# Retention mixer: decay tables made head by head in place, plain gate blocks at both ends, and query/key pairs in a row

## The reference

```python
q, k, v, g = jnp.split(a @ w_in, [hk, 2 * hk, 2 * hk + hv], axis=-1)
q, k = apply_rope(q, *rope), apply_rope(k, *rope)   # latent tokens
k = k * RET_DK ** -0.5
log_gamma = -jnp.exp(decay_param)                   # one per head and direction
o_ctx, o_lat = bidirectional_scan(ctx_terms, lat_terms)
y = rms_norm_2(o)
return (jax.nn.silu(g) * y) @ w_out
```

## Time and profile before

| what | value |
|---|---|
| median of 3 runs | 2966.15 us (2964.76 to 2968.64) |
| profiled execution, own time | 2970.24 us |
| its span, first to last instruction | 2968.4 us |
| mean granted TensorE clock | 0.971 |
| busy: PE, DVE, ACT, POOL | 94%, 68%, 43%, 12% |

### The profile page before, as it was taken

One profiled execution on the slowest core, in us unless ns is written; L12 is line 12 of the kernel. 1 busy time (PEld: TensorE's weight loads), 2 busy tenths in 40 slices (PEclk: granted clock), 3 DMA queues, 4 the chain that ended last, 5 costly groups with the idle time before them and its releaser, 6 DMA issues.

```text
span 2968.4 us, 42896 instructions
## 1 busy us (share of the span) xinstructions
PE 2782.5 (94%) x16374; PEld 2488.8 (84%) x16374; DVE 2023.3 (68%) x3722; ACT 1283.5 (43%) x2369; POOL 369.4 (12%) x207
## 2 busy tenths in 40 slices
PE   9999999999999399989997899999989998999998
PEld 8888987988888298978886889999977777989898
DVE  7788688769878567744546687666674435677676
ACT  5322357633235444432223634334446435554354
POOL 2243200124330000011110000000002222000000
PEclk9999999999999699999998999999989999999999
DMA  6556321256552333323321012222222121122322
GB/s 198 192 182 198 121 95 50 84 190 202 184 161 67 135 137 142 116 104 131 131 96 50 16 59 71 70 71 65 80 71 75 47 72 49 65 79 72 114 86 79
DMA packets 99613, 312.19 MB, mean 105 GB/s; under 512 B 10320, under 2 KB 25808, under 8 KB 97872
## 3 DMA queue, kind: packets, MB, share of 16 engines
q1 hardware_dynamic: 92208, 287.42, 29.7%
q10 hardware_dynamic: 7200, 22.02, 2.0%
HBM read 283.71 MB, written 24.12 MB: 104 GB/s over the span
## 4 chain that ended last, share of the span: by engine, by line
PE 51%; DVE 6%; ACT 2%; issue 1%; DMA 1%; POOL 0%; DVEq 0%; ACTq 0%; SPq 0%; POOLq 0%
PE ps L2248 16%; PE ps L2249 16%; PE ps L2250 16%; DVE t_wlo L2974 1%; PE ps L2531 1%; PE ps L2515 1%; PE ps L2504 1%; ACT t_whi L2574 1%; DVE t_x L3208 0%; DVE t_m L3208 0%; DVE t_m L3093 0%; DMA t_m<-s_dec 0%; DMA t_raw<-in_gu 0%; DVE t_x L3174 0%; DVE t_h L3214 0%
## 5 line engine op out<-in xcount | busy, mean ns | idle before, releaser
L2574 ACT CAST t_whi<-t_raw 128x512 fp32r<-128x512 f32 (+3 forms) x494 | 381.4, 783 | 671.5 <-PE ps L2250 457.4
L2248 PE MATMUL ps<-t_h,t_whi 128*128 128x256 f32 (+2 forms) x1852 | 628.3, 339 | 7.7 <-DVE t_wlo L2974 2.6
L2249 PE MATMUL ps<-t_h,t_wlo 128*128 128x256 f32 (+2 forms) x1852 | 623.6, 337 | 0.0
L2250 PE MATMUL ps<-t_h,t_whi 128*128 128x256 f32 (+2 forms) x1852 | 623.6, 337 | 0.0
L2974 DVE TENSOR_TENSOR t_wlo<-t_raw,t_whi 128x512 fp32r<-128x512 f32 (+3 forms) x420 | 356.9, 861 | 121.2 <-ACT t_whi L2574 116.7
L2248 PEld LDWEIGHTS ps<-t_h,t_whi 128*128 128x128 f32 x1852 | 354.7, 192 | 42.2 <-issue 9.9
L2249 PEld LDWEIGHTS ps<-t_h,t_wlo 128*128 128x128 f32 x1852 | 354.8, 192 | 26.1 <-issue 0.2
L2250 PEld LDWEIGHTS ps<-t_h,t_whi 128*128 128x128 f32 x1852 | 354.6, 191 | 26.3
L2248 PE MATMUL ps<-t_mw,t_whi 128*128 128x256 f32 (+2 forms) x922 | 299.3, 325 | 74.6 <-ACT t_tmp L2579 34.8
L2248 PE MATMUL ps<-t_hid,t_whi 128*128 128x256 f32 (+2 forms) x1032 | 335.5, 325 | 0.7 <-DVE t_hid L3273 0.6
L2249 PE MATMUL ps<-t_hid,t_wlo 128*128 128x256 f32 (+2 forms) x1032 | 333.6, 323 | 0.0
(11 more groups left out here) (373 smaller groups left out, 4962.5 us busy)
## 6 DMA issues: line engine op xcount, KB each, us to landing
t_raw<-in_gu SPq DMA_DIRECT2D x174, 512.0 KB, 3.4
t_raw<-in_ada SPq DMA_DIRECT2D x96, 512.0 KB, 3.6
t_raw<-in_dn SPq DMA_DIRECT2D x52, 512.0 KB, 4.2
t_raw<-in_dn SPq DMA_DIRECT2D x24, 384.0 KB, 3.4
s_qk<-t_hid ACTq DMA_DIRECT2D x12, 768.0 KB, 4.3
t_hid<-s_qk SPq DMA_DIRECT2D x6, 1536.0 KB, 11.6
t_raw<-in_ret_v SPq DMA_DIRECT2D x16, 512.0 KB, 4.8
t_raw<-in_ret_g SPq DMA_DIRECT2D x16, 512.0 KB, 3.8
```

Of the source, the lines that this page charges most:

```text
L2248: e.matmul(out, whi, xlo, start=first, stop=False, skip_group_check=shared)
L2249: e.matmul(out, wlo, xhi, start=False, stop=False, skip_group_check=shared)
L2250: return e.matmul(out, whi, xhi, start=False, stop=last, skip_group_check=shared)
L2574: e.copy(m.block(0, it.slot, n), m.raw(it)).then_inc(*S["hi"].of(j))
```

## The change

- One plain gate block (head 3, channel block 2) stays in front, where there were two; a second one (head 3, block 3) is multiplied behind head 3's last value product. Its silu (`g_late`) writes straight to the place of the gates, and head 3 loads three blocks of gates instead of four.
- Heads come in the order 1, 2, 3, 0, and of each first the two query/key pairs, then the gate pairs (head 3: one).
- No decay table is made in front, stored or loaded again. The distances are loaded (`dist_load`, 768 KB) straight into the table's place, and the table is made there: for head 0 while its gate pairs run, for head h+1 behind the last score of head h. The same operations run (two in another order), five on VectorE and three exps on ScalarE.
- The loads of rope, distances and values move from SyncE's queue to ScalarE's.
- The planner counts transfers as longer, the more so the larger they are (1.3 ns more for each element of a row over 1024), which shifts orders everywhere. In the program ScalarE has 51 table loads, before 40.

```diff
@@ schedule, the planner's costs
-            takes, lasts = 480, 3300
+            takes, lasts = 480, 3300 + 1.3 * max(n - 1024, 0)
...
@@ schedule, retention
-        def plain_gates(h, i):
+        def early_gate(h, c):
...
+        def late_gate(h, c, after):
+            def post(g):
+                put("g_late", h=h, c=c, g=g.id, bank=g.bank, t0=g.t0, n=g.n, after=after)
+            columns([(("ret_g", h * 4 + c), (SLOT,), DC, ("h", 4), [(0, "drain_act", post)])], SEG2[::-1])
...
                 if (t0, i) == (0, 1):
                     finish(h, 512, 256)
-                    gated_values(h, 512, 256)
+                    gated_values(h, 512, 256, range(4 if h < n_head - 1 else 3))
+            if h == n_head - 1:
+                from_bank(4)
+                late_gate(h, 3, ov["oc"])
+                gated_values(h, 512, 256, (3,))
             finish(h, 0, 512)
-            gated_values(h, 0, 512)
+            gated_values(h, 0, 512, range(4))
...
-        for h in range(n_head):
-            late = decays(h, late)
-        put("rope_load", after=[("ret_act", ("ll", n_head - 1))])
-        sides[:] = [late] * 4
-        plain_gates(1, 0)
+        put("rope_load", after=pro)
+        sides[:] = [pro] * 4
+        early_gate(n_head - 1, 2)
...
-        gate_pairs = [(1, 1), (2, 0), (2, 1), (3, 0), (3, 1), (0, 0), (0, 1)]
-        pairs = [(h, w) for h in (1, 2, 3, 0) for w in range(2)]
-        for k, (h, w) in enumerate(pairs):
-            seven_pair("qk", h, w)
-            if k != 3:
-                last = seven_pair("g", *gate_pairs[k - (k > 3)])
+        for h in (1, 2, 3, 0):
+            for w in range(2):
+                seven_pair("qk", h, w)
+            if h == 0:
+                rope_done = sides[0] + sides[1] + sides[2] + sides[3]
+                put("dist_load", h=0, after=rope_done)
+                put("ret_decay", h=0, after=rope_done)
+            for w in range(1 if h == 3 else 2):
+                last = seven_pair("g", h, w)
...
-        put("dec_load", h=0, after=rope_done + [("d_ds", n_head - 1)])
         put("v_load", after=[("ps", last["P6"])])
...
             attend(h)
+            if h < n_head - 1:
+                put("dist_load", h=h + 1, after=[("drain_dve", ("ret_p", h, 0, 5))])
+                put("ret_decay", h=h + 1, after=[("p_lo", (h, 0, 5))])
...
-            from_bank(4)
+            if h < n_head - 1:
+                from_bank(4)
@@ ScalarE
-        e.activation(ll, ta, ACT.Exp).then_inc(*S["ret_act"].of(("ll", h)))
+        e.activation(ll, ll, ACT.Exp).then_inc(*S["ret_act"].of(("ll", h)))
         yield
-        e.activation(gs, d2, ACT.Exp, scale=m.sm(8 + h, 1)).then_inc(*S["ret_act"].of(("g1", h)))
-        e.activation(tb[:, 0:640], d2, ACT.Exp, scale=m.sm(4 + h, 1), bias=m.sm(20 + h, 1)).then_inc(*S["ret_act"].of(("g2", h)))
...
+    def g_late(it):
+        w.wait_ge("ps", it.g)
+        wait_all(it.after)
+        e.activation(m.ret_gate(it.c, it.t0, it.n), m.PS[:, it.bank, 0:it.n], ACT.Silu).then_inc(*S["drain_act"].of(it.g, ("g_late", it.t0)))
```

More of the change, by code:

```diff
@@ L319, in arrange @@
                     end = op.due
-        self.heads_on = next(op.item.id for op in self.ops["sync"] if op.item.kind == "ret_setup")
+        self.heads_on = next(op.item.id for op in self.ops["scalar"] if op.item.kind == "ret_setup")
         return self.run(families)
@@ L1375, in retention @@
         ov, t, sides, staged, stores = {}, {}, [[], [], [], []], {}, {h: [] for h in range(n_head)}
[L1377 to L1381, removed]
         def v_rows(h):
@@ L1516, in finish, with gated_values @@
             put("ret_recip", h=h, t0=t0, n=n)
-        def gated_values(h, t0, n):
-            for c in range(4):
+        def gated_values(h, t0, n, some):
+            for c in some:
                 put("ret_y", h=h, c=c, t0=t0, n=n)
@@ L1557, in retention @@
                 state["h_free"] = [("ps", max(it.id for it in items if it.kind == "group"))]
-                put("dec_load", h=h + 1, after=[("drain_dve", ("ret_p", h, 0, 5))])
                 put("qk_load", h=h + 1, after=[("ret_ps", ("s", h, 0, 5))] + [staged[w] for w in range(2)])
             else:
+                state["h_free"] = [("ps", max(it.id for it in items if it.kind == "group"))]
                 state["acc_free"] = [("p_lo", (h, 0, 5)), ("drain_dve", ("ret_p", h, 0, 5))]
@@ L2183, in serve @@
             e.dma_start(m.at(MMASK, 256), dram["mask1"]).then_inc(*S["d_misc"].of("mask1"))
[L2184 to L2206, removed]
         elif it.kind == "qk_load":
@@ L2813, in ret_decay, with dist_load, v_load, rope_load @@
     def ret_decay(it):
[L2814 to L2815 removed]
+        h = it.h
+        ll, gs, tb = m.at(RST, 896), m.at(RST + 896, 640), m.at(RPA, 896)
         w.wait_ge("ret_dve", ("d3", h))
         wait_all(it.after)
[L2818 removed]
+        e.activation(ll, ll, ACT.Exp).then_inc(*S["ret_act"].of(("ll", h)))
         yield
[L2820 to L2826 removed]
+        e.activation(tb[:, 0:640], gs, ACT.Exp, scale=m.sm(4 + h, 1), bias=m.sm(20 + h, 1)).then_inc(*S["ret_act"].of(("g2", h)))
+        w.wait_ge("ret_act", ("g2", h))
+        e.activation(gs, gs, ACT.Exp, scale=m.sm(8 + h, 1)).then_inc(*S["ret_act"].of(("g1", h)))
+    def dist_load(it):
+        wait_all(it.after)
+        e.dma_start(m.at(RST, 1536), dram["dist"]).then_inc(*S["d_dist"].of(it.h))
+    def v_load(it):
+        wait_all(it.after)
+        w.wait_ge("d_vs0", 0)
+        for part in range(2):
+            o, src = (RVV, RVL)[part], dram["s_v"][part]
+            e.dma_start(m.MW[:, o + 2048:o + 3072].bitcast(F32), src[:, 2048:3072]).then_inc(*S["d_rv0"].of(("part", part), 0))
+        for part in range(2):
+            o, src = (RVV, RVL)[part], dram["s_v"][part]
+            e.dma_start(m.MW[:, o:o + 2048].bitcast(F32), src[:, 0:2048]).then_inc(*S["d_rv1"].of(("part", part), 0))
+    def rope_load(it):
+        wait_all(it.after)
+        e.dma_start(m.at(RCS, 1024), dram["rope"]).then_inc(*S["d_ret"].of("rope"))
     def v_store(it):
```

60 lines of the change are left out of this document (29 added, 31 removed).

## The result

The changed kernel takes 2778.7 us (median of 4 runs, 2777.8 to 2781.4) against 2967.2 us before; the ratio is 0.9367, with an interval of 0.9351 to 0.9383. Forecast were 2891 us and a range of 2864 to 2917. The direction was right, the size was not: −188.5 us for −75.

A forecast was written before the change was run, and what follows sets the result against it. TensorE's work (94% of the span) plus its gaps was taken to bound the kernel; −55 − 9 + 0 − 11 = −75 us from 2970.2 gave 2895, less 4.1: 2891 us, range 2864 to 2917.

The forecast's parts named there:

- What bounds the kernel: Whole kernel: time is TensorE's work, 94% of the span, plus its gaps; waits looked at around the retention mixer.
- drift: Rival, whole program: new transfer costs in the planner shift orders, 11 more table loads; +5 to +14 us; chance 0.08.
- Term 1 and 2: Start of the input products, −55 us, and first scores of head 0, −9 us.
- rows of two: Input products: two query/key pairs in a row cost TensorE time, 4 us for all four places.
- term 2: First scores of head 0: table made in place ends an 8.4 us wait, about 1 us may stay; −9 us.
- decay chain: First input pair: snap copies stand behind the decays, a 29.13 us gap that goes when four decays and stores go.
- Term 3: Inside the heads: decay work delays y by 6 to 8 us, but this is covered; 0, up to +12 us.
- cover: Inside the heads: TensorE runs the next head's value rows meanwhile, hiding a delay of 6 to 8 us.
- Term 4: End of head 3: rest of the output product starts earlier, with the moved gate block paid; −11 us (−27 to 0).
- The table loads: Switches of table counted at 1.28 us each, without the skill's drain of about 1380 ns; with it, 2894 us.

The follow-up runs named there:

- e1: Kernel before, planner's walk following only waits and the order inside a family, so due times reach every operation; 2808.8 us, ratio 0.9463.
- e3: Kernel before, with the two loads of the distances issued by ScalarE instead of SyncE, which removes the planner's circle; 2795.9 us, ratio 0.942.
- e2: Changed kernel, with due times carried back only through as many operations as in the kernel before (7287); 2920.6 us, ratio 0.9842 to the kernel before.
- e6: Changed kernel with the planner's old, flat cost of transfers; 2780.1 us.
- e4: Changed kernel with both plain gate blocks of head 3 in front and no late block; 2770.6 us, ratio 0.9336.
- e7: Changed kernel with both plain gate blocks in front and query/key and gate pairs in turn; 2769.0 us, ratio 0.9327.
- e9: Kernel before, with the distances and also the reloads of the decay tables on ScalarE's queue; 2793.8 us.

## Why the prediction was wrong, step by step

- **What bounds the kernel** was half read. That TensorE's gaps decide was right, but I looked for their causes only in the stretch that the diff names, took the waits of the FFN and the attention for given, and put them into the sum at nothing. They were 88.3 us, the largest error. e1 and e3 bring all of it with the due times and none of the other edits, and e2 loses all but 5 us of it with nothing but the due times cut.
- **What the terms are worth with the old due times** is read from e2, which has every edit. Up to the first sum it is 46.5 us ahead of the kernel before (1282.2 to 1235.7), for a forecast of 64; one gap of 24.96 us is left in the first pair, for low parts of weights (L2979). The end of head 3 is 3.0 us longer (90.3 to 93.3), for a forecast of −11. In all it is 47 us for 75. So the right direction at these places was earned, but the time there comes near the forecast, or beyond it, only together with the due times, and that is luck.
- **The step that failed** is the rival "drift": the planner's part was priced as a loss of 5 to 14 us, and for the wrong cause, its costs of transfers (e6: nothing) and the table loads. That an edit can change whether the planner knows any due time was not asked. The planner's part was a gain, of 142 us (e2, beside all the other edits) to 159 (e1, without them) or 172 (e3, with the distances early as well). The order of ScalarE quoted ahead of the prediction had the sign of it: 24 in-place scalings stood ahead of the casts and the silu that TensorE was waiting for.
- **Term 1 and 2**, −64 us for the way to the first head: measured −81.0 up to its first sum. P1 starts at 955.52 us (forecast 958.9; the gate block ahead of it already begins 3.4 us earlier, at 947.21 us) and the first pair ends at about 974 (forecast 980), so this mechanism holds. The fourteen other pairs end at 1184 us and take some 210 us in place of 222.5, where I had taken 4 us more for the rows of two. The difference is the small waits of every pair, again the order: e3, with its pairs in turn as before, keeps TensorE busy for 198.63 of 200 us there. In term 2 the wait of 8.4 us went, and one of 5.32 us came behind another late transfer, where I had left 1 us: of the 9 us of term 2 some 3 came (8.4 to 5.3 us of wait).
- **That the decay chain is a price of its own** was mostly wrong: in e3 the same four decays, with waits of the same kind for their stores (2.61 us where it was 2.76), leave TensorE no gap over 5 us in the first pairs. The gap of 29 us was a chain put at the wrong place. With due times the tables in front, their reload and the queue of the other loads cost 26.9 us together; I had priced tables and reload at 38 (29 and 9).
- **Term 3**, the heads, at 0: 319.5 to 315.2 us. The cover held, with three exps and a table load more a head.
- **Term 4**, −11 us: −17.9 at the end of head 3. Counted from the last value, the output product of 256 columns ends near V + 21 (forecast 19), and y's last low parts start at 1532.33 us, V + 22 (forecast 24 for their end). VectorE's timeline of the changed kernel, to set beside the earlier trace rows:

```profile
1518.57 3.35 DVE L3579 RECIPROCAL t_tmp<-t_tmp 128x512 f32<-128x512 f32 x1 [1.57 <-ACT t_tmp L2895]
...
1532.33 1.28 DVE L3596 TENSOR_TENSOR t_mw<-t_m,t_mw 128x512 fp32r<-128x512 f32 x2
```

  The order was right and its cause was not: e2 has the late gate block and everything else of the change, and 93.3 us there. The late block itself, which I counted as filling a wait, fills only half of itself: it costs 4.3 us at this place and 8.1 in all (e4).
- **The table loads** cost TensorE nothing that these runs show: there are 11 more of them, and it is idle for 144.5 us less. In the changed kernel the activation again starts right behind the load of 1.28 us, as it does (within 0.1 us) for 45 of the 51, and the load right behind the copy ahead of it (ScalarE's timeline):

```profile
1171.54 0.48 ACT L2562 COPY t_tmp<-ps 128x384 f32<-128x384 f32 x1 [1.59 <-PE ps L2233]
1172.04 1.28 ACT L2801 ACT_TABLE_LOAD   x1
1173.34 0.95 ACT L2801 ACTIVATE t_m<-t_m 128x896 f32<-128x896 f32 x1
```

  So nothing here shows the drain that the Trainium skill ("ScalarE: Activation LUTs", section "What ACT_TABLE_LOAD costs") adds. On this point the sum stands as it was made.

Step by step the kernels read: −171.7 us for the circle undone by moving two loads (e3), −26.9 for the tables in place and the loads of rope and values (e7), +9.7 for the late block and the rows of two. That these add up to the measured gain is no check, since each step starts where the last one ends; what tests the first step is e1, 159 us with no load moved, and e2, 142 us lost with the loads where the change has them. What stays open is how much of the 26.9 us belongs to the tables and how much to the queue of the values. By place, the windows give 11.5 us of idle time to the start and 6.2 to the first head.

## What to carry to other kernels

Where a program's order comes from a planner, check first that the planner knows what it should: how many operations have a due time, and whether work that nobody waits for stands ahead of work that is waited for. A change near such a planner can move every stage behind it, and the waits of stages that the diff doesn't touch belong in the sum, at least as a rival. And an edit that comes together with such a cure has to be timed on its own: here two edits that cost 9.7 us together were hidden inside a gain of 188.

## What the runs showed of the hardware

A quarter of the gain is TensorE's clock. The same 16374 matmuls were busy 47.1 us less, at a mean granted clock of 0.998 instead of 0.971. Behind the gaps of 18 and 29 us a matmul of 384 columns took 0.66 us and elsewhere 0.34, and these gaps are gone.

A transfer that comes early does not help if the next one is as late as before. In e9 the table was issued 11.4 us earlier than in e3, and TensorE's wait went from 6.2 us for the table to 4.7 us for the values.
